# RWKV inverse: the copies of T out of PSUM shared between ScalarE and VectorE, one bank each

## What is computed

```python
def step(s, inp):
    rt, wt, kt, vt, at, bt = inp
    sa = jnp.einsum('bhij,bhj->bhi', s, at)
    s = s * wt[:, :, None, :] + sa[..., None] * bt[:, :, None, :] + vt[..., None] * kt[:, :, None, :]
    y = jnp.einsum('bhij,bhj->bhi', s, rt) if with_out else None
    return s, y
```

## Time and profile before

| what | value |
|---|---|
| time before, median of 3 runs | 3816.41 us (3808.62 to 3836.09) |
| the profiled execution | 3810.66 us |
| its span | 3808.8 us |
| TensorE busy | 3161.6 us, 83% |
| VectorE, ScalarE, GpSimd busy | 1503.5, 889.6, 310.0 us |
| stage of the RWKV chunks | 1228 to 1740 us of the span |

### The profile page before, as it was taken

One profiled execution on the slowest core, in us unless ns is written; L12 is line 12 of the kernel. 1 busy time (PEld: TensorE's weight loads), 2 busy tenths in 40 slices (PEclk: granted clock), 3 DMA queues, 4 the chain that ended last, 5 costly groups with the idle time before them and its releaser, 6 DMA issues. The chain is left out here.

```text
span 3808.8 us, 94209 instructions
## 1 busy us (share of the span) xinstructions
PE 3161.6 (83%) x41870; PEld 2289.6 (60%) x41870; DVE 1503.5 (39%) x2488; ACT 889.6 (23%) x1492; POOL 310.0 (8%) x262
## 2 busy tenths in 40 slices
PE   5886579998687878786896985756799999999996
PEld 2765468885365666674883874644356666666663
DVE  0436743332544554555561696544211111111111
ACT  1214322221222434341441442111110111111110
POOL 0011200000120223130000011400000000000000
PEclk7998789998798999997997987887899999999998
DMA  9130012224424010101458440002599999999993
GB/s 370 67 105 10 2 45 92 107 89 179 177 99 174 25 42 20 48 4 42 145 198 311 144 146 1 1 28 75 227 411 411 410 410 410 410 410 411 411 409 115
DMA packets 219569, 684.75 MB, mean 180 GB/s; under 512 B 25200, under 2 KB 50032, under 8 KB 186432
## 3 DMA queue, kind: packets, MB, share of 16 engines
q1 hardware_dynamic: 190720, 652.85, 44.0%
q10 hardware_dynamic: 28608, 28.33, 2.2%
HBM read 660.16 MB, written 20.97 MB: 179 GB/s over the span
## 5 line engine op out<-in xcount | busy, mean ns | idle before, releaser
L3230 PE MATMUL experts_psum_gu<-ring,experts_x 128*32 128x256 f32 x9216 | 507.9, 381 | 18.3 <-ACT experts_x L3274 18.1
L3230 PEld LDWEIGHTS experts_psum_gu<-ring,experts_x 128*32 128x32 f32 x9216 | 296.4, 111 | 220.7 <-ACT experts_x L3274 19.0
L3334 DVE TENSOR_TENSOR experts_gate<-experts_psum_gu,experts_bias 128x768 f32<-128x768 f32 x32 | 30.6, 957 | 866.0 <-PE experts_psum_gu L3230 866.0
L3253 PE MATMUL experts_psum_down<-experts_weights,experts_hiddenT 128*32 128x256 f32 x6144 | 339.1, 380 | 4.1 <-ACT experts_hiddenT L3282 4.1
L3253 PEld LDWEIGHTS experts_psum_down<-experts_weights,experts_hiddenT 128*32 128x32 f32 x6144 | 200.1, 110 | 137.2 <-issue 5.9
L770 PE MATMUL mlp_psum_bank<-mlp_x_high,mlp_w_high 128*128 128x512 f32 (+1 forms) x512 | 175.2, 342 | 13.7 <-DVE xT_rounded L328 13.7
L302 DVE TENSOR_TENSOR ring_rounded<-ring,mlp_w_high 128x1024 fp32r<-128x1024 f32 x128 | 156.7, 1225 | 51.0 <-ACT mlp_w_high L297 51.0
L770 PE MATMUL mlp_psum_bank<-xT_rounded,mlp_w_high 128*128 128x512 f32 (+1 forms) x512 | 175.0, 342 | 0.0
L770 PE MATMUL mlp_psum_bank<-mlp_x_high,ring_rounded 128*128 128x512 f32 (+1 forms) x512 | 173.5, 339 | 0.0
L3230 PE MATMUL experts_psum_gu<-xT,experts_x 128*32 128x256 f32 x3072 | 171.6, 379 | 0.0
L3278 ACT ACTIVATE experts_sigmoid<-experts_gate 128x768 f32<-128x768 f32 x32 | 27.0, 843 | 615.2 <-DVE experts_gate L3336 615.2
(11 more groups left out here) (649 smaller groups left out, 5863.0 us busy)
## 6 DMA issues: line engine op xcount, KB each, us to landing
ring<-in_w_gu SPq DMA_DIRECT2D x186, 1024.0 KB, 13.5
experts_weights<-in_w_down SPq DMA_DIRECT2D x128, 1024.0 KB, 14.9
ring<-in_ada_w SPq DMA_DIRECT2D x36, 2048.0 KB, 12.0
ring<-in_mlp_w SPq DMA_DIRECT2D x32, 2048.0 KB, 8.2
xT<-in_w_gu SPq DMA_DIRECT2D x64, 1024.0 KB, 14.1
ring<-in_w_in SPq DMA_DIRECT2D x12, 2048.0 KB, 7.5
ring<-in_ab_w_in SPq DMA_DIRECT2D x6, 2048.0 KB, 9.8
ring<-in_w_rkv SPq DMA_DIRECT2D x6, 2048.0 KB, 10.5
```

The source lines that it names most:

```text
L3230: mm = nc.tensor.matmul(pg[o, q, gr, :], x, w[:, c:c + C], start=(u == 0 and gr != 1), stop=(u == U - 1), skip_group_check=True)
L3253: mm = nc.tensor.matmul(pd[o, gr, :], hidT[:, ch, gr, GROUP * v:GROUP * v + GROUP], w[:, ch, C * c:C * c + C], start=(v == 0 and ch == 0 a ...
L3334: v.tensor_tensor(gt[:, :, :], pg[:, 0, 0:GROUPS, :], rep(bias[:, 0, :], GROUPS), ALU.add).then_inc(s_bg, 1)
```

## The change

The copy of T is split. ScalarE copies bank 0 (slices 0 to 3 of T) and VectorE bank 1 (slices 4 to 7), each 128x256, at every level from 1 on and in both lanes. Each copy increments `s_tc`, and `level_yx` waits for two increments. VectorE's two copies (both lanes) stand at the head of a level, ahead of its Y additions and behind the preparation that ends the level before.

```diff
                 def level_yx(k, l):
-                    take(s_tc[l])
+                    take(s_tc[l], 2)
                     take(s_xc[l])
...
                     for k in range(1, HALF_LEVELS):
                         for l in range(2):
                             take(s_t[l])
-                            nc.scalar.copy(pair(T[l][:, :, :]), banks[l][:, 0:2, 0:256]).then_inc(s_tc[l], 1)
+                            nc.scalar.copy(T[l][:, 0:4, :].rearrange("p a c -> p (a c)"), banks[l][:, 0, 0:256]).then_inc(s_tc[l], 1)
...
                     for k in range(HALF_LEVELS):
+                        if k:
+                            for l in range(2):
+                                take(s_t[l])
+                                v.tensor_copy(T[l][:, 4:8, :].rearrange("p a c -> p (a c)"), banks[l][:, 1, 0:256])\
+                                    .then_inc(s_tc[l], 1)
                         for l in range(2):
                             take(s_yr[l])
```

## The result

The changed kernel takes 3840.01 us (median; 3831.19 to 3849.13), the kernel before, run beside it, 3822.82 us: ratio 1.0046, 95% interval 1.0036 to 1.0057, **17.2 us slower** (0.0046 x 3823 = 17.6; interval 14 to 22). The profiled execution has a span of 3835.5 us.

A forecast was written before the change was run, and what follows sets the result against it. TensorE sets the pace, and the copies make it wait for VectorE's preparations: 9.1 + 3.9 - 1.4 + 6.1 - 0.5 = +17.2 us, less 2 for gaps, +15; forecast 3828 us, range 3808 to 3848.

The forecast's parts named there:

- k=2, +9.1: Level 2, seven steps: VectorE's copies queue behind mix_k, so level_yx starts 1.3 us late each time, +9.1 us.
- k=3, +3.9 for bonus(): Level 3, four steps with outputs: the copies queue behind bonus(), 0.97 us late on average, +3.9 us.
- k=4, -1.4: Level 4, seven steps: ScalarE's shorter half copy lets TensorE start 0.2 us earlier, -1.4 us.
- k=5, +6.1: Level 5: the copies queue behind scale, making level_yx and solve late in most steps, +6.1 us.
- Last step, -0.5: Last step, with no preparation in front of the copies: three waits shorter by 0.17 us, -0.5 us.
- The 2 us off for TensorE's gaps: TensorE's 43 gaps in which it waited for no one partly absorb the delays: 2 us off the sum.
- VectorE's copy at 0.42, ScalarE's at 0.375: Time of each 128x256 half copy of T in us, estimated from rows of the profile.
- The waits: TensorE's waits for T: 14 to 18 for VectorE over 0.7 us, seven for ScalarE at k=4 of 1.1 to 1.6.
- (a): Rival: TensorE's gaps swallow the delays, time between 3811 and 3817 us; chance 0.12.
- (b): Rival: the split is faster, as it looks, because TensorE's ten waits for T shrink, 3804 to 3814 us; chance 0.08.
- (c): Rival: slower by over 1%, VectorE's copies doubling in time beside GpSimd's masks, 3862 us; chance 0.04.
- (d): Rival: the change doesn't do what it says, for instance two engines in one bank; chance 1 in 100.

The follow-up runs named there:

- e2: The change undone at level k=2 alone, where ScalarE copies T whole as before: 3828.70 us, ratio 1.0005 to the kernel before.
- e10: The kernel before with T split at level k=2 alone, ScalarE copying it whole at all other levels: 3844.19 us, ratio 1.0057.
- e7: The change with T split only at k=4 and at all levels of the last step, elsewhere copied whole by ScalarE: 3818.18 us, ratio 0.9991.
- e8: The change with VectorE's preparation of the next step spread out in smaller pieces: 3820.57 us, ratio 1.0002 to the kernel before.
- e5: The change with both halves of T copied by ScalarE, in two instructions: 3825.14 us, ratio 0.9991 to the kernel before.
- e9: The kernel before, T copied whole by ScalarE, with VectorE's preparation spread out in pieces: 3823.54 us, ratio 1.0005.
- e1: The change with VectorE's copies of T moved ahead of its preparation of the next step: 3866.49 us, ratio 1.0099 to the kernel before.
- e6: The change, filled version: 20 useless TensorE matmuls in the k=2 wait, behind totals; 3838.58 us, ratio 1.0046 to the kernel before.

## Why the prediction was right

**The size and the reason held, the size with some luck.** 15 us were forecast as the likeliest, 17.2 measured (14 to 22). As a time, 3828 was given and 3840 measured; most of that is the base, since the kernel before came out at 3822.8 over more runs and not at the 3816.4 or 3810.7 from which I had counted: 3822.8 + 15 would be 3838. The measurement tells 0.46% from no change (0.36% to 0.57%); the prediction had thought that a difference under 1% could hardly be told.

- *k=2, +9.1*: +9.3 in four traces. By the times this place alone carries the change: without it (e2) nothing that they can show is left, with it alone (e10) all of it is there. By the traces it is the largest part and not all: e2 still has +10.5, at k=3 and k=5.
- *k=3, +3.9 for bonus()*: +4.0 in e2, where nothing else is in it. In the change itself k3 was 7.3 to 10.1; the excess of 3.3 to 6.1 is the clock, a term that is missing from the sum. The two do not simply add up: only two of the four expected waits at k=3 are in the change's trace; in steps 2 and 5, where there is none, TensorE ran at half rate and L2180 of bonus() took 1.23 us instead of 2.17.
- *k=4, -1.4*: -1.5. *k=5, +6.1*: +6.5. *Last step, -0.5*: between -0.3 and +0.5 in the three traces, within TensorE's gaps.
- *The 2 us off for TensorE's gaps*: the rest of the steps came out 1.9 to 3.3 us shorter than before, in the direction expected. It is no evidence for the gaps: e7 and e8, which have no late k=2, show -2.5 and -3.5 there, and e10, which has, +0.4. In e5 and e9, also without it, +2.6 and +0.8 stand there. So no run shows this term. It was taken off and the clock was not counted, and the two work against each other: that 15 lies so near 17.2 owes something to luck.
- *VectorE's copy at 0.42, ScalarE's at 0.375*: 0.422 and 0.372. The estimates from the Trainium skill (VectorE: DVE Perf Modes, The TRN2 errata) were 0.392 and 0.357; the measurement decides, and the rows of this case were nearer in both: 0.42 between its neighbours for VectorE, 0.375 of another copy of the same shape for ScalarE.
- *The waits*: 14 for VectorE, all of over 0.7 us, 17.9 us together, as forecast (14 to 18); the seven at k=4 with 1.3 us on average.

**The rivals.** (a), that the gaps swallow it, is out: at the most they took back 2 to 3 us, not 17. (b), faster, is out where VectorE has work in front of the copy; where it has none (e7) the gain is the 0.2 us a level that was worked out. (c), that the copies double beside GpSimd, is out: 80 copies, 0.414 to 0.426 us. (d) is out: each engine has its 80 copies of 128x256, from its own bank.

**Open.** How the 17 us divide. The order of VectorE's queue as the cause is shown by e5, e7 and e8; the sizes of the single terms are shown in the traces alone. Whether the half-rate stretches cost the timed executions as much as the profiled ones: the traces say 5 us between the change and its filled version, the times 0 and 2. And why e2 and e10, whose parts should add up to the change, come to 2 and 22 us in time (-3 to 7, 16 to 27), where their traces have 10.5 and 16.8 (each sure to some 4 us): what k=3 and k=5 cost does not appear in the times of either.

## What to carry to other kernels

An engine that is idle half of the time is not free at the moment you need it. Before moving work to it, look at what stands ahead of the new instruction in its order, how long that lasts, and when the waiting engine becomes ready; the busy share says nothing about it. If the queue is the trouble, moving the new instruction to its front only hands the wait to what stood there (e1, 38 us); cutting the long piece into parts that fit the gaps (e8) removes it, and then the question is whether the gain was worth anything: here 12.1 us of waits was the most, and most of that was for something else.

## What the hardware showed beside it

- A wait of 1.28 us (0.81 and 1.09 in two of 28 cases) behind totals (16 passes of two columns in 1.95 us) went with TensorE at half rate, 1.2 GHz instead of 2.4, in 18 of the 28, in the wait or behind it (step 3 of the change below): a matmul group of 30 passes took 1.81 us instead of 1.04.
```profile
1465.83 1.81 PE L1907 MATMUL rwkv_psum_lane<-rwkv_X,rwkv_T 64*64 64x64 f32 x30
...
1468.35 1.04 PE L1907 MATMUL rwkv_psum_lane<-rwkv_X,rwkv_T 64*64 64x64 f32 x30
```
Behind the k=4 waits, up to 1.8 us between dense matmuls, there was none before level_yx of k=5 in any of the four traces. Behind the longer ones there was: one of the three of 1.98 us in e8, and all seven of 3.12 to 3.16 us in e1. The Trainium skill (TensorE: Matmul & The Clock Gate, Part 1) says that full rate comes with activity and that an idle TensorE falls back to half; the pair of the change and e6 agrees with it (six of seven steps against one).
- VectorE's 128x1024 products out of SBUF take 1.22 us where GpSimd's masks do not run beside them, and up to 2.18 where they do; how much changes with when they start against the masks. In step 0 of e1, where they start later against the masks, L2169 takes 1.59, L2171 2.18 and L2173 1.22, where it was 1.22, 1.22 and 2.17. The copies out of PSUM keep their 0.42 us (0.414 to 0.427).
